# Turning x, B and y by VectorE and DRAM instead of TensorE in a chunked SSD mixer

## The reference

```
[u|z|xBC|dt] = rms_norm(h) . W_in
u    -> pool mixer (windows 2, 4, 8, 16, then a linear map)
xBC  -> silu(causal conv of width 4) -> x (24 heads of 64), B, C (4 groups of 128)
dt   -> softplus(dt + bias);  a_cs = cumsum(dt * a) within a chunk of 128 tokens
y    = chunked SSD:  per chunk and head
         y_diag = (C B^T * exp(a_cs_i - a_cs_j), causal) . (x dt)
         y_off  = exp(a_cs) * (C . state)
         state  = state * exp(a_last) + B^T . (x dt exp(a_last - a_cs))
y    = rms_norm_per_group((y + d_skip * x) * silu(z))
h   += [pool | y] . W_out
h   += relu(rms_norm(h) . W1)^2 . W2 ;  out = rms_norm(h)
```

## Time and profile before

| what | us |
|---|---|
| median of 3 runs (lowest, highest) | 2666.63 (2663.36, 2667.45) |
| the profiled execution's own time | 2663.49 |
| its span | 2661.8 |
| TensorE busy (matmuls) | 2642.3 |
| VectorE busy | 1661.3 |
| ScalarE busy | 1252.7 |
| GpSimd busy | 1092.2 |

### The profile page before, as it was taken

The page is one execution under the profiler, slowest core; times in us unless marked ns, Lnnn a source line. Parts: engine busy times, 40 slices in busy tenths (PEclk is TensorE's granted clock), DMA queues, the critical chain, the costliest instruction groups (busy, mean ns, idle before and its releaser), DMA issues.

```text
span 2661.8 us, 37490 instructions
## 1 busy us (share of the span) xinstructions
PE 2642.3 (99%) x13962; PEld 2213.7 (83%) x13962; DVE 1661.3 (62%) x2228; ACT 1252.7 (47%) x2526; POOL 1092.2 (41%) x866
## 2 busy tenths in 40 slices
PE   8999999999999999999999999999999999999998
PEld 6888788888888888898888888888888888888887
DVE  6788615788157882377853576564445765666667
ACT  4667653666236672256634455554545222222223
POOL 2133440335003350033443688665655535353434
PEclk9999999999999999999999999999999999999999
DMA  9977666744558536575473655673436742423323
GB/s 335 303 259 244 240 243 248 241 175 179 216 184 262 189 146 248 202 211 209 167 269 135 225 190 208 249 266 131 173 132 226 295 145 103 164 95 127 119 95 158
DMA packets 278850, 532.70 MB, mean 200 GB/s; under 512 B 63994, under 2 KB 146942, under 8 KB 270606
## 3 DMA queue, kind: packets, MB, share of 16 engines
q1 hardware_dynamic: 278670, 530.31, 56.6%
HBM read 384.31 MB, written 145.95 MB: 199 GB/s over the span
## 4 chain that ended last, share of the span: by engine, by line
PE 96%; SPq 1%; DMA 1%; DVE 1%; issue 0%; ACT 0%; POOL 0%; POOLq 0%; ACTq 0%
PE bank L2260 23%; PE bank L2228 22%; PE bank L1849 21%; PE bank L1956 13%; PE bank L1936 8%; PE bank L2040 2%; PE bank L2002 1%; PE bank L2057 1%; PE bank L2020 1%; PE bank L2028 1%; DMA w_scr<-w_both 1%; PE bank L2008 1%; SPq L730 0%; PE bank L1968 0%; PE bank L2015 0%
## 5 line engine op out<-in xcount | busy, mean ns | idle before, releaser
L1849 PE MATMUL bank<-hnT_hi,w_ring 128*128 128x512 f32 x1152 | 367.0, 391 | 0.0
L2260 PE MATMUL bank<-w_first,T_hi 128*128 128x512 f32 x896 | 275.8, 389 | 0.0
L2390 DVE SCALAR_TENSOR_TENSOR acc<-pre,par,acc 128x512 f32<-128x512 f32 x240 | 211.4, 881 | 82.6 <-ACT pre L1365 76.8
L1849 PEld LDWEIGHTS bank<-hnT_hi,w_ring 128*128 128x128 f32 x1152 | 216.2, 188 | 44.7 <-ACT win_tmp L1494 0.5
L2756 DVE TENSOR_TENSOR acc_th<-bank,acc_th 128x512 f32<-128x512 f32 x224 | 150.0, 685 | 157.5 <-PE bank L2260 156.6
L2228 PE MATMUL bank<-T_hi,w_both 128*128 128x512 f32 x768 | 242.5, 389 | 0.5 <-DVE ff L2697 0.5
L1956 PE MATMUL bank<-w_ring,T_hi 128*128 128x512 f32 x768 | 239.0, 392 | 0.0
L1849 PE MATMUL bank<-hnT_lo,w_ring 128*128 128x512 f32 x576 | 224.4, 390 | 0.0
L2260 PEld LDWEIGHTS bank<-w_first,T_hi 128*128 128x128 f32 x896 | 168.2, 188 | 34.9
L1936 PE MATMUL bank<-w_ring,hnT_hi 128*128 128x384 f32 x768 | 195.8, 335 | 1.3 <-DMA w_ring<-w_scr 1.3
L1849 PE MATMUL bank<-hnT_hi,w_both 128*128 128x512 f32 x544 | 182.0, 406 | 0.9 <-ACT pre L1365 0.9
(11 more groups left out here) (316 smaller groups left out, 6255.4 us busy)
## 6 DMA issues: line engine op xcount, KB each, us to landing
w_ring<-w_scr SPq DMA_DIRECT2D x312, 512.0 KB, 4.3
T_scr<-stage SPq DMA_DIRECT2D x32, 1792.0 KB, 6.7
w_scr<-w_both SPq DMA_DIRECT2D x100, 512.0 KB, 4.2
pair_raw<-in_w_ff SPq DMA_DIRECT2D x36, 1024.0 KB, 5.5
third<-T_scr SPq DMA_DIRECT2D x28, 1024.0 KB, 4.9
pair_raw<-T_scr SPq DMA_DIRECT2D x28, 1024.0 KB, 4.8
sums<-sums_scr SPq DMA_DIRECT2D x64, 384.0 KB, 4.9
raw<-in_w_in SPq DMA_DIRECT2D x36, 512.0 KB, 6.5
```

The source lines that it names most:

```text
L1849: mm = nc.tensor.matmul(bank[s][:, :], w[:, k, :], t[:, k, :], start=(k == 0 and j == 0), stop=(k == KT - 1 and j == 2))
L2260: mm = nc.tensor.matmul(bank[4 * half + t][:, :], a[:, k, tok], w[:, k, :], start=(SECOND[q % 7] not in GOES_ON and k == 0 and j == 0), st ...
L2390: ins = nc.vector.scalar_tensor_tensor(acc[:, s, 0:TB], pre[:, s, k:k + TB], w, acc[:, s, 0:TB], ALU.mult, ALU.add)
```

## The change

In blocks 2 to 4, TensorE no longer turns x and B of groups 2 to 4 (12 steps of four transposes a block) nor y of groups 1 to 3 (12 steps of three).

- **x and B.** `finish` writes the product to `pre` (for B to its tile in `F`), and VectorE then turns the 32x32 blocks of the 128x512 tile (one `transpose`, four a group). ScalarE stores the turned tile to DRAM (`store_turned`, behind the evac of the unit two later), and SyncE loads two chunks at a time into `xt`, four DMAs in pieces of 128 bytes (`load_tokens`). All readers of `xb` read `xt` instead; in steps that TensorE still turns, ScalarE makes one copy of 128x512 instead of two.
- **y.** VectorE turns y of step q-2 in `y_turning`, ahead of `y_finish`; once four steps are there SyncE stores 128x12x128 to DRAM and loads it back (`store_y`, `load_y`). The high and low parts are then made once for a group, 128x1536 wide (`y_group_high`, `y_group_low`), at steps 9 and 13 (counted from 0) and behind the mixer, in place of four `y_high` and `y_low` of 128x384.
- **h.** Of the sixteen stores of the turned h eight stay behind unit 16 and eight go behind unit 24.
- `zs` and the places of some buffers move, and semaphores are shared by name. No instruction is added or taken on GpSimd.

```diff
 evac(b, v) on ScalarE:
+    evacuate(b, v, s, ps)
+    store_turned(b, v - 2)
+def store_turned(b, v):
+    n = unit_of(b, v) if b and v >= ITEMS_G else None
+    if n is None or n >= U_POOL or n % UNITS_G not in (0, 2, 3, 4):
+        return
+    g, j = divmod(n, UNITS_G)
+    act.dma_start(xt_scr[b, g, :, j - 2 if j else 3].rearrange("c p n -> p c n"),
+                  turn_tile(g, j).rearrange("p (c n) -> p c n", n=P)
+                  ).then_inc(xt_stored.sem if j else b_stored.sem, 16)
...
+def load_tokens(b, g, pair):
+    xt_stored.wait(sp, b, 48 * g)
+    b_stored.wait(sp, b, 16 * g)
+    q0 = (g - 1) * CH + 2 * pair + 1
+    xw_ready.wait(sp, b, q0 + 1)
+    ty_ready.wait(sp, b, q0 + 1)
+    cols = slice(2 * pair, 2 * pair + 2)
+    blocks = xt_scr[b, g, cols].rearrange("c t (i a) (j f) -> j a (c t i) f", a=32, f=32)
+    for j in range(4):
+        sp.dma_start(xt[32 * j:32 * j + 32, cols, :].rearrange(
+            "p c (k f) -> p (c k) f", f=32), blocks[j]
+            ).then_inc(xt_loaded[pair].sem, 16)
...
+                        if b and n == 24:
+                            store_y(b, 0)
+                            hT_stored.wait(sp, b - 1, 128)
+                        if b and n in (16, 24):
+                            for t in (0, 1) if n == 16 else (2, 3):
                                 store_turned_h(b - 1, t)
+                        if b and n == 24:
+                            load_y(b, 0)
+                        if b and n == 32:
+                            store_y(b, 1)
+                            load_y(b, 1)
+                        if b and g >= 2 and j == 0:
+                            load_tokens(b, g - 1, 0)
+                        if b and g >= 2 and j == 4:
+                            load_tokens(b, g - 1, 1)
...
 slot1 on TensorE:
-                    xb_ready.wait(pe, b, q - 1 if q else 0)
-                    for i, j in enumerate((2, 3, 4, 0)):
-                        mm = nc.tensor.transpose(bank[4 + q % 2][:, i * P:(i + 1) * P],
-                                                 group_tile(g, j)[:, cols], ident[:, :])
-                    mm.then_inc(xb_ps.sem, 1)
+                    if x_by_pe(b, q):          # b == 0 or q < CH
+                        ... the same five lines
...
-                        if q > 1:
+                        if q > 1 and turned_by_pe(b, q - 2):   # b == 0 or q - 2 >= 12
                             y_transposes(b, q - 2)
...
 finish on VectorE:
+                        dst = group_tile(g, 0) if j == 0 else pre[:, s, 0:TB]
+                        steps.link(nc.vector.scalar_tensor_tensor(dst, pre[:, s, 0:TB], 1.0,
+                                                                  acc[:, s, 0:TB], ALU.add,
+                                                                  ALU.mult))
+                        nc.vector.transpose(turn_tile(g, j), dst).then_inc(up_out.sem, 1)
...
+                def y_turning(b, q):
+                    g, c = divmod(q, CH)
+                    yn_ready.wait(dve, b, q + 1)
+                    nc.vector.transpose(y_turn[:, 3 * g:3 * g + 3, c, :],
+                                        y[:, :].rearrange("p (i f) -> p i f", f=P)
+                                        ).then_inc(y_turned.sem, 1)
 y_finish:
+                    if b and 0 < q <= LAST_GROUP:
+                        y_turned.wait(dve, b, q)
...
+                def y_group_low(b, g):
+                    y_group_hi.wait(dve, b, g + 1)
+                    tiles = (slice(None), slice(4 + 3 * g, 7 + 3 * g), slice(None))
+                    nc.vector.tensor_tensor(T_lo[tiles], y_raw[:, 3 * g:3 * g + 3, :],
+                                            T_hi[tiles].bitcast(F32), ALU.subtract
+                                            ).then_inc(y_group_lo.sem, 1)
...
+                        if b and q in (9, 13):
+                            y_group_low(b, q // CH - 2)
                         taps(b, n2[0])
```

More of the change, by code:

```diff
@@ L753, in _ @@
                     meta_pair(j)
-                initial = [s for s in signals if s.start and s not in (state_ready, ffn_loaded, *sums_loaded)]
+                initial = [s for s in signals if s.start and s not in (state_ready, ffn_loaded, xb_ps, xb_ready,
+                                                             b_hi_ready, *sums_loaded)]
                 for j in range(4, POOL_PAIR):
@@ L2165, in after_mixer @@
                         if t == 0:
-                            xb_ready.wait(pe, b, STEPS)
+                            xb_ready.wait(pe, b, CH if b else STEPS)
                         elif t == 2:
@@ L2177, in _ @@
                                 pool_lo.wait(pe, b, 4)
+                            if b and d == 0 and u in (0, 3):
+                                y_group_lo.wait(pe, b, 2 + u // 3)
                             if d == 0 and u == 6:
-                                yT_lo.wait(pe, b, STEPS)
+                                yT_lo.wait(pe, b, CH if b else STEPS)
                             if d == 0:
@@ L2633, in _ @@
                     finish(b, pending)
+                    if b:
+                        y_group_low(b, GROUPS - 2)
                     for i in range(4):
```

182 lines of the change are left out of this document (135 added, 47 removed).

## The result

The changed kernel takes 2685.36 us (median of 4 runs, 2685.01 to 2687.42) and the kernel before, timed beside it, 2665.34 us (2663.36 to 2667.45). The ratio is 1.0077, with a 95% interval of 1.0064 to 1.0089: slower by 20 us. The profiled execution took 2685.35 us with a span of 2683.6; before it was 2663.49 and 2661.8. So 21.8 us are to be found in the trace. The forecast was 2679, with the three mixers 13 us longer.

What follows compares the result with a forecast made beforehand. TensorE bounds the kernel, with VectorE nearly equal in steps 1 to 3. A block: 0.5 + 1.8 + 3.7 - 0.4 - 3 x 0.42 = 4.3 us longer, 13 in three, giving 2679 us; range 2654 to 2694.

Steps and rivals of the forecast that it cites:

- the two waits: TensorE idle before step 3's y_offset product and step 4's state product: about 5 us in group 2, 7 in group 3.
- the first case: VectorE sets steps 1 to 3 at about the forecast sizes; 2672 to 2685 us, chance 0.45.
- TensorE's saving: Transposes leaving TensorE: 0.42 us for y and 0.49 for x and B, twelve each a block; 32.8 us in three.
- The fourth rival: Wide low parts contended beside GpSimd: 4.2 us for 128x1536, 2.3 more a block, 2686 us; chance 0.15.
- y_low's hole: Dropping y_low (0.54 us) gains VectorE only 0.07 a step, as xw_low waits for ScalarE's copy; at most 0.47.
- Group 2: Step 3's yo 2.7 us later against 0.85 margin: state product 1.8 later, 0.42 back at the next group's start.
- Group 1: Four x transposes and one of y: step 3's yo 1.4 us later against 0.91 margin, state product 0.5 later.
- Group 3: The 1.8 us of the group before it plus 1.9 for the wide low part in its second step: 3.7 later.
- the term of the transfers: SyncE issues 18.3 us of DMAs in a 17.0 gap, weights 1 to 2 late; taken as nothing, bounds 0 to 3 a block.
- Late loads: Weights behind 17 DMAs, or xt not landed: TensorE stands 5 to 10 us a block more, 2695 to 2710; chance 0.08.
- All of TensorE's time coming back: VectorE late without holding anything: 2634 us in full, 2661 in a partial case; chance 0.19 in part or whole.
- the margin argument: In group 2 the state product of step 4 starts 0.85 us after yo ends, TensorE's whole margin over VectorE.

Runs made afterwards that it cites:

- h_early: Changed kernel with all sixteen stores of the turned h behind unit 16 again; 2680.9 us, ratio 1.0068 against before.
- h_rows: Changed kernel with the h stores written as rows of 4096 bytes instead of pieces of 128, same places and count; 2681.4 us, ratio 1.0062 against before.
- x_only: Changed kernel with y turned by TensorE again, only x and B by VectorE, all h stores behind unit 16; 2659.7 us, ratio 0.9984 against before.
- x_12_4: x_only with twelve h stores behind unit 16 and four behind unit 24; 2657.46 us, ratio 0.997 against before.
- y_only: Changed kernel with x and B turned by TensorE again, only y by VectorE, all h stores behind unit 16; 2670.5 us, ratio 1.0022 against before.
- low_at_11: h_early with the wide low part of group 1's y at q = 11 instead of 9; 2683.6 us, ratio 1.007 against before.
- h_rows_low11: h_rows with the wide low part of group 1's y at q = 11; 2687.3 us, ratio 1.0082 against before.
- both_reordered: Changed kernel with h stores spread behind units 16 to 22, low part at q = 11, state_add and yo earlier in third steps; 2695.4 us, ratio 1.0113 against before.
- y_low_11: y_only with the wide low part of group 1's y at q = 11 instead of 9; 2668.1 us, ratio 1.001 against before.

## Why the prediction was right, and by what it was short

The sign, the engine and the two waits were right; the size was short by 8.6 us in the three mixers (13 against 21.6). Two of the five cases came true together, VectorE's waits and late weights, and a cost that no case had, the slow clock behind waits, came on top. The time of 2685.4 lies at the upper end of the first case's own range, 2685.

**TensorE's saving.** 0.91 us a step was forecast from starts inside a chain; the step without a wait is 13.97 - 13.28 = 0.69 us shorter (0.33 for y, as 13.98 to 13.65 in group 1; the rest for x). A sequence of short transposes is worth less when it goes than the distance between their starts. This entered the sum only through the three group starts and group 4.

**Transposes.** 128x512 was put at 0.70 us and 128x384 at 0.56. The groups of instructions (count, busy us, mean ns):

```profile
L2611 DVE STREAM_TRANSPOSE y_turn<-y 128x384 f32<-128x384 f32 x36 | 20.4, 568 | 0.0
L2561 DVE STREAM_TRANSPOSE F<-pre 128x512 f32<-128x512 f32 x27 | 19.2, 711 | 0.9
L2662 DVE TENSOR_TENSOR T_lo<-y_raw,T_hi 128x1536 fp32r<-128x1536 f32 x9 | 16.2, 1803 | 0.0
```

Right, and so is the wide low part: 1.8 us against 2.0. The fourth rival, 4.2 us for it, did not come: the nine take 1.74 to 1.92. It was not for want of a meeting. In groups 3 and 4 GpSimd's ty runs beside the low part and takes 2.4 to 2.5 us instead of 1.4:

```profile
951.28 1.74 DVE L2662 TENSOR_TENSOR T_lo<-y_raw,T_hi 128x1536 fp32r<-128x1536 f32 x1
951.44 2.44 POOL L1247 TENSOR_TENSOR ty<-ty,yo 128x384 f32<-128x384 f32 x1 [2.88 <-DVE yo L2780]
```

Here GpSimd paid and not VectorE. The low part of b_both, which the prediction also named, went from 0.28 us to 0.51 in the second and third steps of group 2.

**y_low's hole.** VectorE waits for ScalarE's copy of xw where y_low stood (timeline, group 2 step 1, the same in each step):

```profile
873.84 0.56 DVE L2646 TENSOR_TENSOR xw_both<-xw,xw_both 128x384 fp32r<-128x384 f32 x1 [0.59 <-ACT xw_both L1557]
```

From the end of xw to xw_low it is 0.58 us, and it was 0.59 before. That was the step with 0.07 us of gain, and it is right. It also is why VectorE is at 92 to 93% of steps 1 to 3 (12.32 of 13.28, 12.33 of 13.28, 11.60 of 12.62) and not over 95% as forecast: the other waits are gone, this one is new.

**Group 2.** Forecast 1.8 - 0.42 = 1.4 us longer, 57.6 for four steps; measured 1.21 and 57.4. VectorE begins the group here:

```profile
865.16 0.56 DVE L2631 TENSOR_TENSOR y<-bank,ty 128x384 f32<-128x384 f32 x1 [5.64 <-PE bank L2164]
```

From there to the state product it is 906.47 - 865.16 = 41.31 us, where it was 897.76 - 857.92 = 39.84: 1.5 us later, forecast 1.8. TensorE's two waits are 3.45 us and not the 5.0 forecast, since less was saved.

**Group 1.** The state product of step 4 was forecast 0.5 us later and came 0.9 later behind the group's first C.B. The 0.42 that the next group's start should give back makes the forecast 0.1 for the whole group, and 0.94 was measured: it went into a wait of 0.55 for ScalarE's copy behind yo that I had not seen.

**Group 4.** Forecast 0.4 shorter, measured 0.38.

**Group 3, the step that failed.** Forecast 3.7 - 0.42 = 3.3 longer, measured 5.43. (My "about 59.5 us" for its four steps was a slip: they took 50.8 before, so the forecast stands for 54.1; they took 56.2.) What failed is the term of the transfers, taken as nothing with 3 us as the upper bound. The wait for weights costs 2.0, 3.0 and 2.5 us and the slow clock behind it 1.65 each: 3.6, 4.7 and 4.2 us a block, 12.5 in all. Two parts of it were mis-sized. A store of h took 1.45 us to issue and not 0.94, with y's store and ScalarE's stores in flight beside it (that they are the reason was not tested alone), while the loads of y and xt took the time forecast, 5.66 and 4.14 us against 5.6 and 3.8; and I counted a wait as its own length, without the clock behind it. The reason given for taking nothing was wrong too: the weights are wanted in the group's first step, and the 3.7 us by which TensorE would be late come in its third and fourth. In exchange the pause let VectorE catch up, so the low part cost little in the changed kernel; h_early and h_rows, without the pause, show it: 54.0 and 54.3 for group 3, against the 54.1 forecast.

By the numbers h_early and h_rows are the kernel that I had forecast, 2680.9 and 2681.4 against 2679, but that is partly luck. In h_rows no weights are late and the three mixers are 17.4 us longer than before; about 7 of it is the slow clock, which is in four steps (an estimate, each of them less the same stretch at the full clock in another block or in the changed kernel). So VectorE's waits less TensorE's saving are about 10 us, where I had 13, and the clock, for which I had nothing, filled the rest.

**The rivals.** Late loads, at 0.08, came true in place but at 4.2 us a block instead of 5 to 10, and by the stores of h and not by slow loads. All of TensorE's time coming back was wrong for the change but right for groups 2 to 4 of its half x_only, and the margin argument was wrong there: I had yo 1.7 us later in group 2 by the transposes of x, against 0.85 of margin. x_12_4 shows no wait in groups 2 to 4. In its group 2 (windows of steps 1 to 3):

```profile
857.00:870.59 13.59, 13.59 (x87) 11.36 (x84) 13.11 (x20) 8.67 (x25) 6.38 (x7) 1.00 0.99 268
870.59:884.18 13.59, 13.59 (x87) 11.37 (x83) 13.22 (x21) 9.24 (x26) 6.58 (x7) 1.00 0.65 240
884.18:895.18 11.00, 11.00 (x87) 10.71 (x83) 10.67 (x19) 7.75 (x21) 5.08 (x6) 1.00 0.85 217
```

VectorE is busy 37.0 us, hardly more than the 36.8 of the earlier trace rows, with 2.84 us of transposes in it. The rest of its work became cheaper: xdt and xw of the second step run in 0.55 us each,

```profile
876.24 0.55 DVE L2750 TENSOR_TENSOR xdt<-xt,dtt 128x384 f32<-128x384 f32 x1
876.71 0.55 DVE L2754 TENSOR_TENSOR xw<-xt,dte 128x384 f32<-128x384 f32 x1
```

while in the changed kernel xw in the same step takes 1.18, beside GpSimd's product of the state:

```profile
884.87 0.83 POOL L1235 TENSOR_TENSOR ty<-xt,dsk 128x384 f32<-128x384 f32 x1
885.78 1.22 POOL L1238 TENSOR_TENSOR S<-S,cd 128x384 f32<-128x384 f32 x1
886.24 1.18 DVE L2767 TENSOR_TENSOR xw<-xt,dte 128x384 f32<-128x384 f32 x1
```

Before, xw took 1.18 in the second and the third step too (the earlier trace rows have the third). In x_12_4 that product begins only at 878.02, and what runs beside xw is ty, which pays itself:

```profile
876.70 1.25 POOL L1226 TENSOR_TENSOR ty<-xt,dsk 128x384 f32<-128x384 f32 x1
878.02 1.07 POOL L1229 TENSOR_TENSOR S<-S,cd 128x384 f32<-128x384 f32 x1
```

So of two instructions that meet either may be the longer one. The Trainium skill, "SBUF — State Buffer", Who interferes with whom, says that an instruction of VectorE with two SBUF inputs contends with a GpSimd one that reads SBUF, and that one with at most a single SBUF input, outside the 2-port modes, doesn't. The trace agrees in both: all 36 transposes of 128x512 took 0.71 us, and xw or ty is stretched where they meet. I had taken the durations of before as fixed; they moved by more than the margin that I compared them with. That this shift is the whole reason why x fits was read from traces and not tested by a run of its own.

**The halves don't add.** x_12_4 is 7.7 us faster than before and y_only 5.6 slower, a sum of 2 faster; the changed kernel is 20 slower. Each half alone fits nearly into VectorE's room in steps 1 to 3; together they don't, and their transfers meet in one gap of SyncE's. Moving single results helped little: in low_at_11, h_rows_low11 and group 1 of both_reordered the wait came back elsewhere. That VectorE's sum alone is the limit is not shown, though, for group 3 of both_reordered came near its time before; its order without the spread stores was not run.

## What to carry to other kernels

Moving work off the bounding engine pays only as far as the receiving engine has room in the same stretch: take the halves apart, since here one gained 8 us and the other lost 6. DMAs with small pieces are work for the issuing queue; put them into its idle gaps, count them there with the issue time that they have in traffic, and never in front of a transfer that the bounding engine waits for. When a time is forecast by a margin of under 1 us, the durations of contended instructions are no constants. And a wait of the bounding engine is priced with the clock behind it, which here was as large as the wait in several steps.

## What the runs showed of the chip

**A short wait can cost twice.** In y_only the third step of group 3 has the same wait in two blocks, 1.78 and 1.79 us for s_both, and takes 13.14 us in one and 14.70 in the other. The windows behind the waits:

```profile
604.53:608.50 3.97, 3.97 (x23) 3.97 (x24) 3.66 (x6) 1.76 (x5) 2.78 (x4) 1.00 0.99 274
...
949.96:953.93 3.97, 3.97 (x15) 3.96 (x16) 3.65 (x6) 1.77 (x5) 2.77 (x4) 0.64 0.97 282
```

In the second TensorE runs mostly at 1.2 GHz, 15 products instead of 23, and loses 1.55 us. The same sum of about 1.6 us stands behind all three waits for weights in the changed kernel and behind one of its waits for s_both; the other waits of 1.7 us had none. Which waits draw it differs from block to block and stays open. Over the mixers it is in no step of before, x_only, x_12_4 and y_low_11, where no wait is longer than 0.7 us, and in one to five steps of each kernel with longer waits. That it is also why executions of one kernel differ by a few us (h_early 2678.64 to 2687.51) is likely and not shown, since only one execution of each was profiled.

**The issue time of one DMA form varies more than tenfold.** A store of 1024 pieces of 128 bytes took 0.31 to 4.80 us of SyncE over all kernels here. The first of a row took 0.43 in most cases, and the nine above 4 us all stand second or third of four behind loads of weights. With pieces of 4096 bytes the eight took 6.04 us together instead of 11.60.
